# Compressed attention, retention and the turning of the latent heads in one stage; adaptation spread out; two norms in one stage

## The reference

```
# first block, two layers (l = 0, 1)
h = rms_norm(x, ln1_gain[l]);  proj = h @ w_in[l]                # 1024 x 2866
o_nsa = compressed attention + selected blocks + window          # 6 heads of 64
o_mla = attention over latents (q, k, v by small products)       # 5 heads
o_ret = silu(gate) * groupnorm(retention(q, k, v)) * gain        # 5 heads
x = x + concat(o_nsa, o_mla, o_ret) @ w_out[l]
x = x + square(relu(rms_norm(x, ln2_gain[l]) @ w_up[l])) @ w_down[l]
x = rms_norm(x, final_gain)                                      # end of first block
# second block, layers ab and cd; xc is the context
shift, scale, gate = split(silu(c) @ w_ada + b_ada)              # 1024 x 3072: "adaptation"
cshift, cscale, cgate = the same with c_ctx
h  = rms_norm(x, g) * (1 + scale) + shift;   hc = the same of xc
ab: u = h @ w_in; conv over 31 taps with layer norm; attention with axial rope
    x = x + gate * ((concat(y_a, y_b) * silu(z)) @ w_out);  xc likewise
cd: Fourier mixing and neighbourhood attention with a bias table (rpb)
    x = x + gate * ((concat(y_c, y_d) * silu(z)) @ w_out)
return rms_norm(x, final_norm_g)
```

## Time and profile before

| what | value |
|---|---|
| median of three runs | 1237.38 us |
| the profiled execution | 1240.61 us |
| its span | 1238.8 us |
| mean granted TensorE clock over the span | 0.982 |
| TensorE busy | 1173.4 us (95%) |
| VectorE busy | 769.0 us (62%) |
| ScalarE busy | 545.7 us (44%) |
| GpSimd busy | 41.3 us (3%) |
| mean from HBM and to it | 147 GB/s |

### The profile page before, as it was taken

The page is one execution under the profiler, slowest core; times in us unless marked ns, Lnnn a source line. Parts: engine busy times, 40 slices in busy tenths (PEclk is TensorE's granted clock), DMA queues, the critical chain, the costliest instruction groups (busy, mean ns, idle before and its releaser), DMA issues. The chain is left out here.

```text
span 1238.8 us, 19484 instructions
## 1 busy us (share of the span) xinstructions
PE 1173.4 (95%) x7600; PEld 1016.0 (82%) x7600; DVE 769.0 (62%) x1454; ACT 545.7 (44%) x953; POOL 41.3 (3%) x45
## 2 busy tenths in 40 slices
PE   7988999999999998999999999899999999999996
PEld 6876868988987885877999899798887888988865
DVE  4574635655555464646787888679966644653474
ACT  4533534544444442634444444353547421533362
POOL 1000000000000000000100000000210000000000
PEclk9999989999999998799999999999999999999998
DMA  9538064555555546154555565333341022473101
GB/s 351 193 115 339 2 248 160 189 186 184 190 170 175 180 154 245 62 200 146 179 193 185 170 201 193 123 122 106 101 115 30 18 69 68 88 265 103 34 2 51
DMA packets 51647, 182.92 MB, mean 148 GB/s; under 512 B 17636, under 2 KB 30308, under 8 KB 31972
## 3 DMA queue, kind: packets, MB, share of 16 engines
q1 hardware_dynamic: 51556, 181.68, 44.0%
HBM read 178.78 MB, written 2.89 MB: 147 GB/s over the span
## 5 line engine op out<-in xcount | busy, mean ns | idle before, releaser
L219 DVE TENSOR_TENSOR w_lo<-ring,w_hi 128x1024 fp32r<-128x1024 f32 x264 | 322.1, 1223 | 249.0 <-ACT w_hi L213 247.0
L213 ACT CAST w_hi<-ring 128x1024 fp32r<-128x1024 f32 x264 | 275.2, 1051 | 355.6 <-PE banks L250 343.5
L250 PE MATMUL banks<-f_hi,w_hi 128*128 128x256 f32 x512 | 144.8, 283 | 0.5 <-DVE f_lo L352 0.5
L250 PE MATMUL banks<-f_hi,w_lo 128*128 128x256 f32 x512 | 145.0, 283 | 0.0
L250 PE MATMUL banks<-f_lo,w_hi 128*128 128x256 f32 x512 | 144.4, 282 | 0.0
L250 PE MATMUL banks<-w_hi,u_hi 128*128 128x512 f32 x256 | 101.1, 395 | 0.0
L250 PE MATMUL banks<-w_lo,u_hi 128*128 128x512 f32 x256 | 101.0, 395 | 0.0
L250 PE MATMUL banks<-w_hi,u_lo 128*128 128x512 f32 x256 | 101.0, 394 | 0.0
L281 PE MATMUL banks<-ident 128*128 128x128 f32 x750 | 93.4, 279 | 6.7 <-PEq L298 5.7
L281 PEld LDWEIGHTS banks<-ident 128*128 128x128 f32 x750 | 88.3, 193 | 14.0 <-issue 12.2
L250 PEld LDWEIGHTS banks<-f_hi,w_hi 128*128 128x128 f32 x512 | 96.7, 189 | 1.3 <-DVE f_lo L352 0.8
(11 more groups left out here) (365 smaller groups left out, 2299.7 us busy)
## 6 DMA issues: line engine op xcount, KB each, us to landing
ring<-in_w_up SPq DMA_DIRECT2D x32, 1024.0 KB, 5.2
ring<-in_w_down SPq DMA_DIRECT2D x32, 1024.0 KB, 5.1
ring<-in_w_in SPq DMA_DIRECT2D x24, 1024.0 KB, 5.1
ring<-in_ab_ada SPq DMA_DIRECT2D x12, 1024.0 KB, 6.4
ring<-in_cd_ada SPq DMA_DIRECT2D x12, 1024.0 KB, 5.7
ring<-in_cd_in SPq DMA_DIRECT2D x12, 1024.0 KB, 6.3
ring<-in_w_out SPq DMA_DIRECT2D x8, 1024.0 KB, 7.6
ring<-in_ab_in SPq DMA_DIRECT2D x16, 512.0 KB, 4.7
```

The lines of the kernel that those rows point to most:

```text
L213: nc.scalar.copy(w_hi[:, n % PARTS, :], part_source(key, q)).then_inc(hi_ready, 1)
L219: nc.vector.tensor_tensor(w_lo[:, n % PARTS, :], part_source(key, q), w_hi[:, n % PARTS, :].bitcast(F32), ALU.subtract).then_inc(part_read ...
L250: mm = nc.tensor.matmul(dst, a, b, start=first_one and i == 0, stop=last_one and i == 2, skip_group_check=shares_bank)
```

## The change

The list of weights gets a new order: in each layer of the first block stand three slabs of ab's adaptation (`ada_turn`, `ada_small`, `ada_mix`; both layers together make the six), and the six of cd's stand in layer ab (`cd_heads` 2, `cd_turn` 1, `cd_conv` 3) ahead of `ab_out`. Each is multiplied in the stage of its name, mostly where a filler stood, and its rows are turned four at a time. `transpose_groups` always does one slab behind its transpositions. `retain` and `center_values` are gone; `compressed_attention`, `retain` and the transposition of the latent heads become `compress_and_retain`. Values are centred at the end of `project_and_prepare`, the retention gate is multiplied by its gain in `small_products`. `turn_mixed` splits the first part of the next weights after its first group, and `ab_in` splits nothing ahead of `ab_out`. `out_project` has no turning and no filler at its start. The first block's last norm and ab's first norm share one stage; its gain row is loaded during the last feed-forward. The convolution's padding alone is set to zero, not the whole tile.

```diff
-LAYER_SLABS = [("w_in", W_IN_SLABS), ("cmp_k", 1), ("cmp_v", 1), ("small", 1), ("adapt0", 1), ("adapt1", 2),
-               ("adapt3", 3), ("w_out", 2), ("ffn", 16)]
+LAYER_SLABS = [("w_in", W_IN_SLABS), ("ada_turn", 1), ("cmp_k", 1), ("cmp_v", 1), ("small", 1), ("ada_small", 1),
+               ("ada_mix", 1), ("w_out", 2), ("ffn", 16)]
-SECOND_SLABS = [("ab_in", 6), ("ab_out", 2), ("cd_in", 6), ("cd_out", 2)]
+SECOND_SLABS = [("ab_in", 6), ("cd_heads", 2), ("cd_turn", 1), ("cd_conv", 3), ("ab_out", 2), ("cd_in", 6), ("cd_out", 2)]
...
+        TURN_AHEAD = [("w_out", layer) for layer in range(DEPTH)] + ["ab_out"]
         def split_own(split, engine, key, q):
-            if key not in next_key.values() or q >= AHEAD:
+            if q >= (1 if key in TURN_AHEAD else AHEAD if key in next_key.values() else 0):
                 split(engine, key, q)
...
+            def two_norms_on_vector(dve):
+                for t in tiles:
+                    nc.vector.tensor_tensor(mixed[:, t, :], x[:, t, :], gain, ALU.mult).then_inc(gained, 1)
+                dve.wait_ge(gained, 1)
+                nc.vector.tensor_tensor_reduce(junk(0), mixed[:, 0, :], mixed[:, 0, :], 1.0, 0.0, ALU.mult, ALU.add,
+                                               sums[:, 2:3]).then_inc(squares_summed, 1)
+                dve.wait_ge(gained, 2)
+                dve.wait_ge(norm_rstd, 1)
+                for t in tiles:
+                    nc.vector.tensor_scalar(x[:, t, :], mixed[:, t, :], rstd[:, t:t + 1], None, ALU.mult).then_inc(gained, 1)
+                dve.wait_ge(norm_rstd, 2)
+                nc.vector.tensor_scalar(mixed[:, 1, :], mixed[:, 1, :], rstd[:, 5:6], None, ALU.mult).then_inc(scaled_too, 1)
...
-                    keep_busy(0, 24)
+                    keep_busy(0, 24 if gain is None else 34)
...
# transpose_groups, TensorE: behind the groups
-                    pe.wait_ge(copied1, 1)
-                    keep_busy(1, busy)
+                    if burst_bank < len(groups):
+                        pe.wait_ge((copied0, copied1)[burst_bank % 2], burst_bank // 2 + 1)
+                    adapt_products(pe, key, 0, burst_bank)
...
# out_project, TensorE: at the start
-                    if kind is None:
-                        keep_busy(6, 7)
-                    else:
-                        turn_conditions(pe, 1, 7, turned)
...
# small_products, TensorE: behind the latent products
+                    turn_conditions(adapted(0), banks[:, 7, :]).then_inc(turned, 1)
                     pe.wait_ge(partial_ready, 1)
...
# compress_and_retain, TensorE
+                    scores_of(0)
+                    scores_of(1)
                     for j, (pair, g, t) in enumerate(jobs):
                         mm = nc.tensor.matmul(...)          # compressed scores
+                    mm.then_inc(cmp_scores, 1)
+                    for h in range(2, RET_H):
+                        scores_of(h)
+                    turn_conditions(adapted(1), banks[:, ADA_TURNED, :]).then_inc(turned, 1)
+                    values_of(0)
+                    values_of(1)
                     pe.wait_ge(probs_ready, 1)
+                    pe.wait_ge(ada_ready, 1)
                     for j in range(N):
                         mm = nc.tensor.transpose(...)       # compressed probabilities
+                    for h in range(2, RET_H):
+                        values_of(h)
+                    pe.wait_ge(probs_copied, 2)
                     for j, (pair, g, t) in enumerate(jobs):
                         mm = nc.tensor.matmul(...)          # compressed values
+                    adapt_products(pe, ada_key, 0, ADA)
+                    for g, (blocks, _) in enumerate(groups):          # latent heads
+                        if g >= 3:
+                            pe.wait_ge(heads_copied, g - 2)
+                        ...
+                    pe.wait_ge(kept, 1)
+                    turn_conditions(adapted(2), banks[:, ADA, :]).then_inc(turned, 1)
...
# compress_and_retain, ScalarE: behind the exponentials and the squares
+                    keep_adapted(act, ada_key, 0, ADA, adapted(2)).then_inc(kept, 1)
+                    for g, (_, copies) in enumerate(groups):
+                        act.wait_ge(heads_turned, g + 1)
+                        for copy in copies:
+                            last = copy(nc.scalar, banks[:, TURNED[g % 3], :])
+                        last.then_inc(heads_copied, 1)
...
# turn_mixed, ScalarE (VectorE: split_lo in the same place)
+                        if g == 0:
+                            split_hi(act, key, 0)
...
# prepare_axial_heads
                 def _(sp):
+                    load_behind(sp, "cd_heads", 2)
                     sp.dma_start(rpb_rows[:, OFF_DIAGONAL:OFF_DIAGONAL + N_DC], ...).then_inc(skew_here, 16)
                     sp.wait_ge(skew_here, 16)
                     sp.dma_start(skew..., rpb_rows...).then_inc(skew_here, 16)
                 def _(pe):
                     spread_gates(pe, 0, 2, rows_ready)
-                    keep_busy(7, 20)
+                    for j in range(2):
+                        adapt_products(pe, "cd_heads", j, 4 + j)
+                    for j in range(2):
+                        pe.wait_ge(kept, j + 1)
+                        turn_conditions(cd_rows[:, j, :], banks[:, 6 + j, :]).then_inc(turned, 1)
...
# finish_conv_and_gate, TensorE: behind its transpositions
-                    keep_busy(7, 30)
-                    pe.wait_ge(tanh_y_ready, 1)
-                    keep_busy(7, 36)
+                    for j in range(3):
+                        adapt_products(pe, "cd_conv", j, 4 + j)
+                    turn_conditions(cd_row, banks[:, 7, 0:16])
+                    for j in range(3):
+                        pe.wait_ge(kept, j + 1)
+                        mm = turn_conditions(cd_rows[:, j, :], banks[:, 7, 16 * (j + 1):16 * (j + 2)])
+                    mm.then_inc(turned, 1)
+                    keep_busy(4, 8)
...
         first_block()
-        final_norm(dram["final_gain"], False)
         second_block()
```

More of the change, by code:

```diff
@@ L252, in multiply, with adapt_products @@
             return mm
-        def adapt_products(pe, layer, s, bank, signal=True):
-            place = next(p for p, (a, b) in ADA_HALVES.items() if a <= 2 * s < b)
-            for h in (2 * s, 2 * s + 1):
-                i = first[place, layer] + h - ADA_HALVES[place][0]
+        def adapt_products(pe, key, j, bank, signal=True):
+            for h in range(2):
+                i = first[key] + 2 * j + h
                 w = ring[:, i % SLOTS, :].rearrange("p (k n) -> p k n", k=KC // 2)
@@ L309, in build_program, with norm_programs @@
                         "norm_whole", "norm_low")
-        def norm_programs(signals, hidden, tiles, scales, shifts=None, spare=None, load_rest=None, power=None):
+        def norm_programs(signals, hidden, tiles, scales, shifts=None, spare=None, load_rest=None, power=None, gain=None,
+                          room=None):
             (squares_summed, norm_step, norm_rstd, scaled, scaled_too, x_turned, norm_high, norm_whole,
-             norm_low) = signals
+             norm_low) = signals[0:9]
+            if gain is not None:
+                gained, raw_summed = signals[9:]
             T, per = len(tiles), len(scales)
@@ L356, in on_vector @@
                     return
-                square_on_vector()
-                dve.wait_ge(norm_rstd, 1)
-                for n in others:
+                if gain is not None:
+                    two_norms_on_vector(dve)
+                else:
+                    square_on_vector()
+                    dve.wait_ge(norm_rstd, 1)
+                for n in (others if gain is None else ()):
                     t = tiles[n]
@@ L379, in on_gpsimd @@
             def on_gpsimd(pool):
+                if gain is not None:
+                    two_norms_on_gpsimd(pool)
+                    return
                 step = InOrder(pool, norm_step)
@@ L390, in on_scalar @@
             def on_scalar(act):
-                if shifts is not None:
+                if gain is not None:
+                    two_norms_on_scalar(act)
+                elif shifts is not None:
                     square_on_scalar()
@@ L500, in products_done, with transpose_groups @@
             engine.wait_ge(part_used, first_part[key] + 4 * (s + 1))
-        def transpose_groups(groups, busy, loads=()):
-            with stage("turned", "copied0", "copied1", "tables_here") as (
-                    turned, copied0, copied1, tables_here), nc.Block() as block:
+        def transpose_groups(groups, burst):
+            key, burst_bank, rows = burst
+            with stage("turned", "copied0", "copied1") as (turned, copied0, copied1), nc.Block() as block:
                 @block.sync
                 def _(sp):
-                    for dst, name in loads:
-                        sp.dma_start(dst[:], dram[name]).then_inc(tables_here, 16)
```

(9 more changed lines are left out.)

401 lines of the change are left out of this document (207 added, 194 removed).

## The result

The changed kernel takes 1232.78 us (median of 14 runs, 1226.97 to 1237.68); the kernel before, in the runs beside it, 1239.94 (14 runs). The ratio is 0.9935, 95% interval 0.9912 to 0.9958: 0.4 to 0.9% faster. The forecast was 1212.4, with a range of 1198 to 1228. The direction was right, the size was not: 7 us came of 25.

A forecast was written before the change was run, and what follows sets the result against it. TensorE bounds the kernel, with its fillers, waits and granted clock. Layers -18.0 and -22.2, new half-clock stretches +5, two norms -4.5, second block +14.7: -25.0 from 1237.38 gives 1212.4 us, range 1198 to 1228.

The forecast's parts named there:

- New half-clock stretches in the first block: Both layers: fewer fillers and new thin runs lower the clock, one chance in three per stretch; +5, bounds 0 and 16.
- Merged stage: Compressed attention, head turnings and retention as one stage per layer: 20.0 us, saving 16.4 and 17.2; bounds 18 and 26.
- Rival 3: Merged stage takes 26 us, held by ScalarE's copies and waits between engines: layers +12, 1224.4 us; chance 0.13.
- (a): Centring the values moves to the tail of the w_in stage, unhidden: +1.95 us, bounds 0 to 2.5.
- (b): Filler beside the head turnings becomes a slab of adaptation with a copy behind it: +0.1 us.
- (c): Four turnings of conditions stand in the small products ahead of the hidden product: +0.95 us, layer 1 +1.15.
- (d): `turn_mixed` takes the first split, 1.65 us longer, but `out_project` starts its products at once: -2.05 us in both layers.
- (e): First output products run at full clock instead of half: -2.2 us in each layer.
- (f): Layer 1's attention, before at a clock of 0.81, keeps the clock as in layer 0: -3.7 us.
- Heads of ab: Second block's heads stage: the bias table's load lands behind four ring loads and SyncE waits; +10.7 us, bounds 0.5 and 13.
- Rival 2: Clock stays full everywhere except after the second block's heads gap, real products replacing idle time: 1205.9 us; chance 0.12.
- Rival 4: Without fillers the clock falls in the merged stage and stays low through attention: +17, 1254 us, slower; chance 0.07.

The follow-up runs named there:

- fillers_merged: The kernel after with 22 more fillers in each merged stage and 22 instead of 8 at the end of the w_in stage: 1259.18 us, ratio 1.0156.
- fillers_at_ends: second_block with conditions' turnings moved to the stage before the output product, 8 fillers behind them, 18 instead of 8 ending the finish: 1208.91 us.
- skew_later: The kernel after with the second block's skewed write moved to the attention stage and the small load ahead of the ring loads: 1215.18 us, ratio 0.9807.
- second_block: skew_later plus condition turnings ahead of the finish's last adaptation slab and 16 fillers instead of 8 ending the w_in stage: 1213.24 us, ratio 0.9769.
- mixed_again: second_block with conditions' turnings moved before the output product, adaptation in one block between retention scores, value products among head turnings: 1210.45 us.
- mix_merged: The kernel after with the merged stage reordered: adaptation two by two among scores, value products among head turnings, condition turnings before the values: 1243.14 us, ratio 1.0014.
- skew_first: The kernel after with the small load and the skewed write ahead of the four ring loads in the same head stage: 1224.71 us, ratio 0.9858.

## Why the prediction was wrong

- **The step that failed: "New half-clock stretches in the first block", +5 in both layers.** The merged stages alone lost 7.5 and 6.1 us to the half clock (26.90 and 25.46 against the estimate of 19.4), the head turnings 1.7 each (8.56 against 6.89), the first output stage 1.5 (25.85 against 24.31), the attention of layer 1 0.6: 19 us. The mechanism was named, and 19 lies past its upper bound of 16. I had priced it as one chance in three per stretch, from stretches of the kernel before in which fillers stood in the waits. Here it was no chance: in all ten traces of the merged stage the clock fell. The merging runs the thin products, formerly in pieces, on end; that this is what brings the clock down is argued, not shown, and 22 fillers put back among them (fillers_merged) didn't keep it up.
- **Merged stage, 20.0 us.** About right as work at full clock (19.4 by the estimate). Its end was right too: in layer 0 ScalarE's copies end at 131.55, the last turnings at 131.67 and the last bias at 131.9. What was wrong is when that tail begins: the adaptation ahead of it ended 22.1 us into the stage, not 15.5, and up to there TensorE was busy on end, three quarters of it at half clock. Rival 3's 26 us came true as a number and not as a mechanism: fillers_merged speaks against a chain of waits.
- **Terms (a) to (d).** (a) +1.80 for +1.95 (the three steps it names add up to 1.85); (b) +1.85 for +0.1, 1.7 of it half clock; (c) +0.91 for +0.95; (d) -1.76 and -2.1 for -2.05. (e), -2.2 each: -0.6 and -1.8, since in layer 0 the half clock came there again (0.93); fillers_at_ends shows that it was to be had. (f), -3.7: -3.9.
- **Two norms**, -4.5: -4.35. The filler took 7.83 us, as said, but the chain beside it took 8.0 and not 6.7: TensorE idled 0.18 us behind its filler until ScalarE's scaled rows were there. That the two met is luck, and with a shorter filler the stage would hardly have been shorter.
- **Heads of ab**, +10.7: +10.6, with the landing of the small load behind the four ring loads as the cause; skew_later takes it away. This was the sum's largest loss and well founded, on how five loads stood behind each other. The 1.5 us more for the table's small elements has no row behind it: the last ring load landed at about 907.8, and SyncE went on 0.6 us later.
- **What stands behind it was missed.** +2.5 for a cold clock in the turnings was too little, for want of SyncE's second hold: its ring loads stand behind the skewed write (3.00 and 1.91 us to issue them). Term: +4.2, measured +6.9. The attention's +2.9 was not in the sum: I let the clock come back at its start. In the finish VectorE was to set the end, -1.4: TensorE did, +3.0, with its last eight fillers, 3.1 us longer than VectorE. They came late for two reasons: TensorE idled 2.2 us for the last slab's load, and everything behind it ran at half clock. Where the clock held (second_block, 0.98), with the turnings ahead of that slab, VectorE ended the stage and it took 17.32 us, 0.3 over the forecast.
- **Rival 2**, from the Trainium skill (page "TensorE: Matmul & The Clock Gate", section "Why this matters for your kernels"), which asks for no idle gaps over about 3 us, fell: at 108.1 the clock halved with TensorE busy on end, and it stayed at half to 118.3, with no gap in that time. **Rival 4** was the right kind of loss, in its merged stage: there it had 8.0 us at half clock for 2.7 lost in 20, the runs show 13.7 to 20.4. Its second part, an attention that stays cold, only mixed_again shows (34.97 us at 0.78).

What stays open: which mixture of thin and wide products keeps the clock. The same instructions gave 13.7, 17.2 or 20.4 us at half clock from one stage to the other, and no run here varied only that. The spread of the kernel after's runs goes with it: between the fastest and the slowest lie 11 us, and their mean granted clocks were 0.972 and 0.960. That is 30 us more at half clock, or 13 us at the merged stage's 0.44 (an estimate).

## What to carry to other kernels

Before merging stages to remove waits, ask what TensorE did in those waits: a stage of thin products that loses them becomes bound by TensorE, and at a falling clock, so count its instructions at both levels and let the range hold both. Fillers pay only where TensorE waits anyway, and they must fit the wait at half clock too, or they become what ends the stage. Thin work moved into such a wait is hidden, but can carry the half clock into the next stage; eight fillers behind it prevented that here. In a list of transfers of one queue, keep a small load that someone waits for out from behind large ones, and a large write in small pieces away from any load whose issue a stage's end waits for.

## What the runs showed of the hardware

- Sixteen adaptation records of 512 columns that write four partition groups in turn take 1.92 us in a row at full clock; between other products two of them, or four, take 1.04 us (mix_merged).
- A record of 15 columns costs 0.10 us at full clock (24 in 2.40), nearly as much as one of 128 (48 in 5.60, 0.12 each).
- Issuing can take long: the two ring loads behind the skewed write took SyncE 3.00 and 1.91 us, the first one behind it in skew_first 8.1 us, each of four with nothing before them 0.33. Whether the write's bytes or its number of pieces does it, no run shows.
- With 16 or 22 fillers in the wait ahead of the head turnings the clock stayed full in them in ten of ten traces, with 8 in three of fourteen.
